# Norm 1's weight and bias inside other passes, and four memory-value slots among the mixer's output tiles

## The reference, cut to what matters

```python
mix = hybrid_mixer(x, ...)                  # its last step: concat(out_a, out_b, out_c) @ w_out
x = layer_norm(ALPHA * x + mix, ln2_g[l], ln2_b[l])          # "norm 1" in the kernel
# memory_cross_attn(x, mem, w_q, w_kv, w_o):
q = x @ w_q
k, v = split(mem @ w_kv)                    # mem: 256 rows of 1024, the same in both layers
scores = einsum(q, k) * XA_HEAD_DIM ** -0.5
o = einsum(softmax(scores), v)
x = layer_norm(ALPHA * x + o @ w_o, ln3_g[l], ln3_b[l])      # "norm 2"
```

## Time and profile before

| what | value |
|---|---|
| median of 3 runs | 2213.21 us (2211.64 to 2213.45) |
| the profiled execution | 2213.39 us, of which the span of its instructions is 2211.6 us |
| PE busy | 2173.9 us, 98% of the span |
| DVE, ACT, POOL busy | 51%, 37%, 45% |
| HBM read | 207.06 MB, 95 GB/s over the span |

### The profile page before, as it was taken

The page is one execution under the profiler, slowest core; times in us unless marked ns, Lnnn a source line. Parts: engine busy times, 40 slices in busy tenths (PEclk is TensorE's granted clock), DMA queues, the critical chain, the costliest instruction groups (busy, mean ns, idle before and its releaser), DMA issues. The chain is left out here.

```text
span 2211.6 us, 27011 instructions
## 1 busy us (share of the span) xinstructions
PE 2173.9 (98%) x11072; PEld 1817.0 (82%) x11072; DVE 1118.9 (51%) x1221; ACT 821.0 (37%) x1143; POOL 994.9 (45%) x413
## 2 busy tenths in 40 slices
PE   9999999999999999999999999999999999999998
PEld 7888889788778888888888888897786888888887
DVE  4433235987746733323453333369877476333334
ACT  3322224836444522222353222257365345222222
POOL 4444444436443544444364444454265335444443
PEclk9999999999999999999999999999999999999999
DMA  5233332333322233232233333223243222333321
GB/s 180 96 95 98 111 105 60 89 101 105 110 85 66 82 97 96 95 120 92 75 98 100 98 99 107 100 60 94 87 124 105 86 67 78 99 100 96 115 92 51
DMA packets 96043, 210.91 MB, mean 95 GB/s; under 512 B 39344, under 2 KB 52016, under 8 KB 95664
## 3 DMA queue, kind: packets, MB, share of 16 engines
q1 hardware_dynamic: 94944, 208.19, 30.4%
q10 hardware_dynamic: 976, 1.00, 0.1%
HBM read 207.06 MB, written 2.10 MB: 95 GB/s over the span
## 5 line engine op out<-in xcount | busy, mean ns | idle before, releaser
L582 POOL TENSOR_TENSOR w_lo<-raw,w_hi 128x1024 fp32r<-128x1024 f32 (+2 forms) x358 | 930.5, 2601 | 1195.7 <-ACT w_hi L1307 1195.5
L1307 ACT ACTIVATE w_hi<-raw 128x1024 fp32r<-128x1024 f32 (+2 forms) x358 | 401.6, 1122 | 1216.1 <-PE psum L674 1141.0
L668 PE MATMUL psum<-acts_hi,w_hi 128*128 128x512 f32 x1744 | 685.2, 393 | 3.0 <-ACT tmp L1694 3.0
L671 PE MATMUL psum<-acts_lo,w_hi 128*128 128x512 f32 x1744 | 679.6, 390 | 0.0
L674 PE MATMUL psum<-acts_hi,w_lo 128*128 128x512 f32 x1744 | 430.8, 389 | 0.0
L668 PEld LDWEIGHTS psum<-acts_hi,w_hi 128*128 128x128 f32 x1744 | 327.9, 188 | 76.1 <-issue 3.9
L671 PEld LDWEIGHTS psum<-acts_lo,w_hi 128*128 128x128 f32 x1744 | 328.0, 188 | 69.8 <-issue 2.4
L674 PEld LDWEIGHTS psum<-acts_hi,w_lo 128*128 128x128 f32 x1744 | 327.3, 188 | 68.0
L1952 DVE TENSOR_TENSOR work<-work,psum 128x512 f32<-128x512 f32 x85 | 58.4, 687 | 547.1 <-PE psum L674 542.1
L668 PE MATMUL psum<-h_hi,w_hi 128*128 128x512 f32 x616 | 239.6, 389 | 0.0
L671 PE MATMUL psum<-h_lo,w_hi 128*128 128x512 f32 x616 | 239.6, 389 | 0.0
(11 more groups left out here) (307 smaller groups left out, 2495.0 us busy)
## 6 DMA issues: line engine op xcount, KB each, us to landing
raw<-w_in SPq DMA_DIRECT2D x176, 512.0 KB, 3.6
raw<-w_out SPq DMA_DIRECT2D x64, 704.0 KB, 4.0
raw<-w_kv SPq DMA_DIRECT2D x32, 512.0 KB, 3.6
raw<-w_mix SPq DMA_DIRECT2D x26, 512.0 KB, 3.6
raw<-w_q SPq DMA_DIRECT2D x16, 512.0 KB, 3.6
raw<-w_o SPq DMA_DIRECT2D x16, 512.0 KB, 3.6
raw<-w_v SPq DMA_DIRECT2D x4, 768.0 KB, 4.2
raw<-w_mix SPq DMA_DIRECT2D x24, 128.0 KB, 3.2
```

The lines of the kernel that those rows point to most:

```text
L582: nc.gpsimd.tensor_tensor(w_lo[:, n % SPLIT, 0:width], raw[:, n % RAW, 0:width], w_hi[:, n % SPLIT, 0:width].bitcast(F32), ALU.subtract).t ...
L668: nc.tensor.matmul(o, hi, b_hi, start=start and k == 0, stop=False)
L671: nc.tensor.matmul(o, hi, b_lo, start=False, stop=False)
L1307: A(w_hi[:, n % SPLIT, 0:width], raw[:, n % RAW, 0:width], ACT.Copy).then_inc(w_hi_made, 1)
```

## The change

- **Order of slots** (`TAIL`, one table for PE, ACT and SyncE's loads): the mixer's output tiles and the first four value slots are mixed: out 0, out 1, v 0, out 2, out 3, v 1, out 4, v 2, out 5, v 3, out 6, out 7. Behind the last output tile come the statistics and the values 4 to 7, and then the query tiles. The copy of the first half of the values to `v_st` follows v 3.
- **Weight**: DVE's multiplication by the scale becomes `scalar_tensor_tensor`, which multiplies by the weight as well.
- **Bias**: ACT's high part is made from x plus bias in one pass (`Identity` with a bias) and the pass in place is gone; DVE's low part is made by `(x + bias) - high`, again `scalar_tensor_tensor`. x itself gets the bias on POOL (`bias`, 8 instructions a layer), between the weights' splits of the query slots, and DVE's residual of norm 2 waits for them (`x_biased`).
- **Variance, in every norm**: the first difference goes to PSUM (the bank of the first root) and the `tensor_scalar` behind it reads it from there.
- **Bank** of the first query tile: 2 in place of 0.

```diff
+TAIL = [("out", 0), ("out", 1), ("v", 0), ("out", 2), ("out", 3), ("v", 1), ("out", 4), ("v", 2),
+        ("out", 5), ("v", 3), ("out", 6), ("out", 7), ("v", 4), ("v", 5), ("v", 6), ("v", 7)]
+TAIL_SLOT = {e: S_MIXOUT + n for n, e in enumerate(TAIL)}
...
+def q_bank(m):
+    return m % 2 if m else 2
...
@@ gpsimd
+            def bias(layer, k):
+                c = V_LN + 16 + KT + k
+                pool.wait_ge(x_split, x_count(layer, 1, k))
+                nc.gpsimd.tensor_scalar(x[:, k, :], x[:, k, :], vecs[:, c:c + 1], None,
+                                        ALU.add).then_inc(x_biased, 1)
...
-                slots(layer, S_K + 2 + AT, S_IN[1])
+                slots(layer, S_K + 2 + AT, S_Q + 2)
+                for k in range(KT):
+                    bias(layer, k)
+                    if k < KT - 2:
+                        split(layer, S_Q + 2 + k)
+                slots(layer, S_AO, S_IN[1])
@@ tensor
-                out_rest(layer, S_MIXOUT, 1, MIXT, act, 1, KT)
+                for kind, i in TAIL[1:12]:
+                    if kind == "v":
+                        memory_values(layer, i)
+                        continue
+                    if i >= 2:
+                        pe.wait_ge(z_added, z_count(layer, 1, i - 2))
+                    tile_of(layer, TAIL_SLOT[kind, i], bank(i % 2), act, MIXT)
...
-                memory_values(0, 0)
-                memory_values(0, 1)
                 stats_first(layer, 1, 0)
                 stats_rest(layer, 1, 0)
-                memory_values(0, 2)
-                memory_values(0, 3)
                 pe.wait_ge(z_added, z_count(layer, 1, KT - 1))
-                for s in range(4):
-                    memory_values(1, s)
+                for i in range(4, 8):
+                    memory_values(layer, i)
...
@@ scalar
             def attention(layer):
-                step(layer, S_V)
-                step(layer, S_V + 1)
                 square_of_mean(layer, 1, 0)
                 root(layer, 1, 0)
+                step(layer, TAIL_SLOT["v", 4])
+                step(layer, TAIL_SLOT["v", 5])
                 for k in range(KT):
-                    if k in (0, 1, 3, 5):
-                        step(layer, S_V + 2 + (k + 1) // 2)
-                    scaled(layer, 1, k)
-                    if k == 4:
-                        for m in range(2):
-                            A(v_st[:, m, 0:SEQ], bank(V_BANK[0] + m), ACT.Copy).then_inc(kv_read, 1)
-                step(layer, S_V + 6)
+                    if k == 2:
+                        step(layer, TAIL_SLOT["v", 6])
+                    act.wait_ge(y_centered, x_count(layer, 1, k) - KT)
+                    A(act_hi[:, k, :], x[:, k, :], ACT.Identity,
+                      bias=vec(V_LN + 16 + KT + k)).then_inc(x_hi_made, 1)
...
@@ vector
             def variance(layer, n, h, eps):
-                v = var[:, tokens_in(n, h)]
-                V.tensor_tensor(v, square_mean_of(layer, n, h), v, ALU.subtract)
+                v, t = var[:, tokens_in(n, h)], first_root_of(n, h)
+                V.tensor_tensor(t, square_mean_of(layer, n, h), v, ALU.subtract)
                 dve.drain()
-                V.tensor_scalar(v, v, 0.0, eps, ALU.max, ALU.add).then_inc(var_ready, 1)
+                V.tensor_scalar(v, t, 0.0, eps, ALU.max, ALU.add).then_inc(var_ready, 1)
...
-                    V.tensor_tensor(x[:, k, :], x[:, k, :], scale_of(n, 0),
-                                    ALU.mult).then_inc(y_centered, 1)
+                    V.scalar_tensor_tensor(x[:, k, :], x[:, k, :], vec(V_LN + 16 * n + k),
+                                           scale_of(n, 0), ALU.mult,
+                                           ALU.mult).then_inc(y_centered, 1)
...
-                    V.tensor_tensor(act_lo[:, k, :], x[:, k, :], act_hi[:, k, :].bitcast(F32),
-                                    ALU.subtract).then_inc(x_split, 1)
+                    V.scalar_tensor_tensor(act_lo[:, k, :], x[:, k, :], vec(V_LN + 16 + KT + k),
+                                           act_hi[:, k, :].bitcast(F32), ALU.add,
+                                           ALU.subtract).then_inc(x_split, 1)
```

More of the change, by code:

```diff
@@ L196, in pieces @@
 def pieces(s):
-    if S_MIXOUT <= s < S_V:
+    if S_MIXOUT <= s < S_Q and TAIL[s - S_MIXOUT][0] == "out":
         return 2 + HEADS
@@ L553, in _ @@
                 stage(w_kv, layer, S_K, 8, 16)
-                for m in range(KT):
-                    mixed_weights(layer, S_MIXOUT + m, m)
-                stage(w_kv, layer, S_V, 8, 16, 8)
+                for kind, i in TAIL:
+                    if kind == "out":
+                        mixed_weights(layer, TAIL_SLOT[kind, i], i)
+                    else:
+                        load(w_kv, layer, TAIL_SLOT[kind, i], 8 + i, 16)
                 stage(w_q, layer, S_Q, 8)
@@ L950, in ffn @@
                     stats_rest(layer, n, 1)
-            def out_rest(layer, s0, n, units, act, m0, m1):
-                for m in range(m0, m1):
-                    if m >= 2:
-                        pe.wait_ge(z_added, z_count(layer, n, m - 2))
-                    tile_of(layer, s0 + m, bank(m % 2), act, units)
             def mixer(layer):
@@ L1143, in mixer @@
                 pe.wait_ge(kv_read, layer * 12 + 6)
-                tile_of(layer, S_MIXOUT, bank(0), act, MIXT,
+                tile_of(layer, TAIL_SLOT["out", 0], bank(0), act, MIXT,
                         hi_arrived=lambda k: pe.wait_ge(mixed_hi, layer * MIXT + k + 1),
@@ L1175, in q_tile @@
                         pe.wait_ge(kv_read, layer * 12 + 12)
-                    tile_of(layer, S_Q + m, bank(m % 2), act, KT)
+                    tile_of(layer, S_Q + m, bank(q_bank(m)), act, KT)
                 def scores(h):
@@ L1361, in affine @@
                 return A(x[:, k, cols], x[:, k, cols], ACT.Identity, bias=vec(c + 8), scale=vec(c))
-            def scaled(layer, n, k):
-                affine(layer, n, k, slice(0, SEQ))
-                act.drain()
-                A(act_hi[:, k, :], x[:, k, :], ACT.Copy).then_inc(x_hi_made, 1)
             def scaled_pair(layer, n, h, k):
@@ L1800, in raw_lo, with residual @@
                                        ALU.subtract).then_inc(raw_lo_made, 1)
-            def residual(layer, n, s0, per_tile, alpha, between=None, at=lambda m: m % 2):
+            def residual(layer, n, slot_of, alpha, between=None, at=lambda m: m % 2):
                 dve.drain()
                 V.memset(work[:, 0:2, :], 0.0)
+                if n == 2:
+                    dve.wait_ge(x_biased, (layer + 1) * KT)
                 if later(layer, n):
@@ L1810, in residual @@
                         between[m]()
-                    done(layer, s0 + (m + 1) * per_tile - 1)
+                    done(layer, slot_of(m))
                     V.scalar_tensor_tensor(x[:, m, :], x[:, m, :], alpha, bank(at(m)), ALU.mult,
@@ L2193, in keys_lo @@
                                     ALU.subtract).then_inc(kv_split, 1)
-                residual(layer, 1, S_MIXOUT, 1, ALPHA, {3: keys_hi, 5: keys_lo})
+                residual(layer, 1, lambda m: TAIL_SLOT["out", m], ALPHA,
+                         {3: keys_hi, 5: keys_lo})
             def attention(layer):
```

36 lines of the change are left out of this document (22 added, 14 removed).

## The result

The changed kernel takes **2218.77 us** (median of 10 runs, 2216.67 to 2219.97), the kernel before 2213.33 us beside it: ratio 1.0023, 95% interval 1.0015 to 1.0031, so slower by 0.15 to 0.31%. The forecast was 2217.3. The profiled execution took 2217.7 us, 4.3 more than that of before.

The account below looks back on a forecast made before the run. PE, busy 98% of 2211.6 us, was taken as the bound. From 2213.39 us, +2.7 for both layers' stretches, +1.6 for the clock and -0.2 for variances gave 2217.5, or 2217.3 on the median's scale; range 2209.5 to 2221.5.

Parts of the forecast that it names:

- The slots' move: Four value slots among output tiles cost PE 10.88 us there, no new wait; PE through with its slots about D + 11.1.
- D: ACT's square of the mean in each layer's norm statistics, 3.63 us after PE starts them; forecast 5.44 us later than before.
- DVE's chain: In the norm: variance from PSUM +0.26 us, eight multiplications with a weight pointer +0.5; first low part at D + 15.6.
- POOL in the way: POOL's split of query slot 1 holds DVE's fifth low part until D + 21.0; the eighth ends 3.0 us later than alone.
- the rival without it: POOL doesn't hold the low parts: low-weight pass 3.0 us earlier in each layer, 2211.3 us; chance 0.24.
- The bias on POOL: POOL's bias of 512 columns takes about 1.05 us; the first runs before the sixth low part.
- The clock: Half clock on PE from idling before the first low part, in both layers: 0.8 us a layer taken, +1.6 in all.
- the 1.6 that the prediction had as price: Eight matmuls of the low-weight pass losing 0.2 us each at low clock: 1.6 a layer, bounds 0 and 2.0.
- PE's second wait: PE stands again for 2 us between its fourth and fifth tile in the first query tile.
- The low-weight pass: PE's pass of the first query tile after DVE's last low part: forecast to start at D + 24.25.
- The rest: Biases' delay of the softmax +0.0 (bound 0.4 a layer), values' split no later; other variances, last norm, -0.2 us.
- The gain side: Low parts come as PE needs them before the first query tile, both layers' losses go: 2196 us; chance 0.10.

Follow-up runs that it names:

- the slots alone: The new order of slots with the norm's passes as in the kernel before (ACT scales in place, no bias on POOL): 2212.20 us, ratio 0.9995.
- an earlier split: The changed kernel with POOL's biases one slot later and ACT's weight copy of query slot 1 ahead of the sixth high part: 2212.14 us, ratio 0.9992.
- a later one: The changed kernel with biases one slot later, and ACT copying query slot 1's weight only after the last low part: 2214.47 us, ratio 1.0004.
- the matmuls that kept it up: The changed kernel with 29 unread PE matmuls, 20 before the first low activation and 9 before the fifth: 2216.07 us, ratio 1.0013.
- The version with PSUM and slots among the output tiles: The changed kernel's slot order, with high and low parts read from PSUM, POOL making x as high + low, one slot later: 2214.59 us, ratio 1.0007.
- giving two slots of cover back: The changed kernel's norm with six value slots behind the statistics, as in the kernel before: 2210.57 us, ratio 0.9987.
- The version that took 2197.4: Low parts from PSUM with all value slots behind the statistics (2203.45 us), plus value slot 7's weight copied before the seventh high part: 2197.39 us, ratio 0.9929.
- all eight slots behind: The changed kernel's folded passes with all eight value slots behind the statistics, none among the output tiles: 2208.27 us, ratio 0.9977.
- the version with the later bias: The changed kernel with POOL's first bias moved behind the split of query slot 2: 2217.05 us, ratio 1.0016.

## Why the prediction was right

Point by point, by its own steps.

- **The slots' move.** D was to come 5.44 us later and came 5.42 later, and PE was through with its slots at D + 11.2 (D + 11.1 forecast). No new wait among the output tiles. Right, and the run with the slots alone, no slower than before, says so too.
- **DVE's chain.** `tensor_scalar` from PSUM took 0.69, which is 0.26 more than the 0.43 from SBUF, as taken, and the multiplications stood 0.84 apart (four in 3.28); the first low part came at D + 15.58, forecast D + 15.6. PE's wait in front of it was 4.8 us, for DVE's low part (5.3 forecast).
- **POOL in the way.** The split was forecast at about D + 18.0 and came at 613.33, D + 17.93; the fifth low part was ready at D + 21.1 (D + 21.0 forecast), the eighth at D + 23.5 (D + 24.0). Taking the collision away by an earlier split gave 4.9 us, by a later one 2.6; 6.0 was the forecast of the rival without it. That rival's price was about right, and its condition wasn't met: the split fell where the working had put it.
- **The bias on POOL** was mis-sized: 1.57 us alone and 2.00 beside DVE instead of 1.05, since 512 columns took nearly three times what 256 do, not twice. And the step by which the first bias runs before the sixth low part, and makes one of near 1.6 us, was wrong: it runs beside low parts, the sixth took 1.17, and it costs them 0.44 us in all. That is why the eighth low part came 0.5 earlier than forecast.
- **The clock.** It fell in both layers. 0.8 us a layer was taken; it costs 1.1 to 1.2 by the matmuls that kept it up. The sentence that half clock costs little while PE follows DVE is where that was lost: DVE gave the last two low parts 0.66 apart, PE needs 0.86 for two matmuls, so it was 0.6 us behind at the eighth (619.51 against 618.90), and it lost 0.5 more in the low-weight pass (2.49 instead of 1.98). PE's second wait was 1.0 us and not 2 for the same reason: it was itself still at the tiles before. The version with PSUM and slots among the output tiles shows the whole pass at half clock, the 1.6 that the prediction had as price.
- **The low-weight pass** started at D + 24.53 in both layers, D + 24.25 forecast. That it came so near is in part luck: low parts that ended 0.5 early stand against a PE that was 0.8 later behind them than forecast. With the clock's part the sum for query tile 1 was +1.4 and +2.9 us, measured +1.40 and about +3.0.
- **The rest.** -0.2 was taken for the other variances; all that lies outside the two stretches came to about -0.1 in the profiled executions.

The forecast of 2217.3 is 1.5 us under the median. Its sum was made for a profiled execution, 2217.5, and the one that was profiled took 2217.7; that the median lies 1.1 above it no step of the working explains. What the prediction had not seen is the *interaction*: it costed both halves in one sum, and by the expectation for the slots alone (2226) I would have blamed them. The runs of each half alone show that both are harmless or better. The loss needs both: ACT's freed time lets POOL start while DVE writes low parts, and with four slots behind D nothing covers what that adds. Taking the collision away gives 6.6 us (2218.77 to 2212.14, with the bias later), and giving two slots of cover back gives 8.2 (2210.57).

The gain side was costed at 2196 for low parts that come as PE needs them. The version that took 2197.4 got there another way, with all eight value slots behind D, so the nearness of the two numbers bears out what PE had lost before (9.3 and 7.8 us), not the change.

## What to carry to other kernels

An engine made faster lets its followers start earlier; before freeing one, list what they then run beside. Cover that brings work for a third engine with it (here a split of 2.4 us for every slot) can delay what it is to cover. Where two engines take turns at SBUF, putting one operand of the critical engine in PSUM can be worth more than the order of the work: 14.0 us here, with the same instructions in the same order and full cover, against 11.1 for the order of the slots with that norm.

## What was unexpected of the hardware

- A POOL instruction with one tensor input and a pointer (`tensor_scalar`, 128x512) does not hold DVE's two-input instructions: 2.00 us instead of 1.57 for itself, and 0.44 in all for the low parts beside it. A two-input split made one take up to 2.88 us (all eight slots behind).
- DVE's cast between two SBUF tensors (128x2048) took 1.21 us with POOL idle and 3.04 beside a split, though it has one input.
- PE at half clock in pursuit of DVE stayed there for about 10 us in the changed kernel, PE fully busy in all but three windows of it. In the version with the later bias full clock came back in layer 0 in the window (616 to 617) in which PE's pause of 1.1 us began; in layer 1 such a pause passed at half clock, which lasted some 4 us longer. What decides between the two wasn't found.
